# Key preparations, state reload, gated blocks and last root in other places, and the second mixer's fine levels on four 32-column tiles

## The chip, the cores and the metric

One core of a Trainium2 chip runs the whole program. The metric is the device time of one execution in microseconds; of several runs the median counts. TensorE (PE) multiplies, VectorE (DVE) and ScalarE (ACT) read its results out of PSUM banks and prepare operands, SyncE (SP) issues the loads of weights, and ScalarE issues most other DMAs from its own queue. Each engine works through its instructions in the order in which they were written; semaphores hold the engines together.

## The reference

One inference step of a decoder layer, for 512 prompt tokens and 8 x 8 sample tokens of width 1024, in fp32. Cut to what matters here:

```python
def gla_scan(q, k, v, la, S0):                 # second mixer, chunked
    def step(Sst, inp):
        Bc = jnp.cumsum(lac, axis=1)
        decay = jnp.exp(where(tril, Bc[:, :, None] - Bc[:, None, :], -inf))
        A = jnp.einsum('bthd,bshd,btshd->btsh', qc, kc, decay)
        o = einsum('btsh,bshv->bthv', A, vc) + einsum('bthd,bhdv->bthv', qc * exp(Bc), Sst)
        S_new = exp(BL)[..., None] * Sst + einsum('bshd,bshv->bhdv', kc * exp(BL[:, None] - Bc), vc)
...
def trunk(...):
    a = rmsnorm(h); z = a @ w_in                # all projections of both mixers
    hm = mlstm_scan(mq, mk, mv, li, lf)         # first mixer: matrix memory
    hg = gla_scan(gq, gk, gv, la, S0)           # second mixer: gated linear attention
    merged = sigmoid(ga) * (head_layernorm(hm) * sigmoid(mo) @ w_pa) + sigmoid(gb) * (head_rmsnorm(hg) * silu(gg) @ w_pb)
    h = h + merged @ w_o
    h = h + conv_ffn(rmsnorm(h))
    h = h + sigmoid(rmsnorm(h) @ w_ple_gate) * (p @ w_ple_proj)
    y = rmsnorm(h)
```

The outputs are the tokens and, for both mixers and the convolution, the states after the prompt and after the sample tokens.

## The kernel before

**Order.** `plan()` writes the whole order down as one list, `sched`. Its units are slices of weights: each is loaded by SP (`wraw`), split by ScalarE into a rounded high part (`whi`, L1841) and by VectorE into the rest (`wlo`, L1117, or in halves, L1125), and used by TensorE in tiles of 128 output features (or of 128 tokens for the values `mv`, `gv`). Each tile is three sums of fast products, high by high, low by high and high by low (L750 and, where the low weights are awaited first, L756; L859 and L865 for the values; L777 to L786 for the last projection). Between the tiles the list places stages, small steps of the mixers and norms. All engines walk the same list, and each does its part of a stage where it stands. The dictionaries in `plan()` say behind which tile of a unit a stage comes. Stages take jobs in the four PSUM banks of `aux`, in turn from `bank0`, except `m1`, which always takes banks 0 to 3; TensorE waits with `bank(j)` until the bank's last user has been read.

**First mixer.** A prompt chunk is 128 tokens (`c` 0 to 3; `NC` = 4 is the sample). `m1 c` makes key transposes, scores and spread rows on TensorE (L950 to L958), and VectorE and ScalarE weight them. `m2 c` multiplies keys by values (L969, VectorE adds to the state) and the scores by the values (L975, L979), which ScalarE copies out (L1917). For the sample rows `hpre`, `hout` and four `hk` update the states `st` in two pairs of heads: each `hk` takes all four banks (L1013), VectorE updates (L1784), and ScalarE stores that part of the state (L2112); for the first pair of a mixer it then reloads the part before with the next pair's state (L1912), after a wait for its store.

**Second mixer.** The decay between two tokens of a chunk is cut into levels of width 64, 32, ..., 1: at each level queries and keys are scaled relative to the middle of blocks of twice the width (`lsub`, `lmul`), and TensorE multiplies the early half of a block by the late one (`lev`, L1050 for 64, L1056 for the others, `gkt` L1032 for the diagonal). The levels go in pairs, four `lev` stages a chunk. Two 64 x 64 diagonal blocks, on two 64-column tiles of the array, hold all levels under 64; VectorE collects them through masks in `attd` (L1713), ScalarE copies `attd` into `att` (L2146), and `gout` multiplies by the values (L1066 to L1075).

**Gated blocks.** `bt m n` and `bt g n` transpose a mixer's output (L910, L912), gate it (VectorE L1808 to L1812, ScalarE L1879, L2168, VectorE L1178) and so make block n of the inputs of the units `pa` and `pb`. `pa`'s tiles are multiplied by their gate from PSUM (L1212).

**Last norm.** The last projection `pgate` runs over tokens 256 to 575, then over 0 to 255 (`PLE_ORDER`). `rsum 3` sums the squares of the first part, `rroot 3` takes the root (ScalarE L1844, VectorE L1149 to L1159) and `rspread 3` spreads it over the partitions (TensorE L717, L719). For tile g `evac` (L1297) takes the product out, `merge_ple` and `sum_square` handle the tile before, and `lo_half` (L1125) splits half a unit's weights.

## Time and profile before

| | us |
|---|---|
| median of 3 runs | 1207.81 |
| all runs | 1207.75, 1211.03, 1207.81 |
| profiled execution | 1210.15 |
| its span in the profile | 1208.4 |

| engine | busy us | share of the span |
|---|---|---|
| TensorE, products | 1184.1 | 98% |
| VectorE | 739.1 | 61% |
| ScalarE | 371.1 | 31% |
| GpSimd | 2.3 | 0% |

The span runs from the first to the last instruction; the profiled execution is some 2 us longer than its span, and above the median of the runs. TensorE's busy time is the union of its products, so overlapping ones count once. Every fp32 product stands in the trace as two passes, each with a weight load (PEld) of its own; those with rounded operands are one. All times below are us from the start of the span in the profiled execution.

### The profile page before, as it was taken

The page shows a single profiled execution, that of the slowest core. Times are in us where ns is not written, and L with a number is a line of the kernel's source. Part 1 is how long each engine was busy: PE and PEld are TensorE (multiplying, and loading weights), DVE is VectorE, ACT ScalarE, POOL GpSimd, SP SyncE. Part 2 cuts the span into 40 slices and gives each one's busy share as a digit, 9 for nine tenths or more (in the row PEclk, how much of TensorE's full clock was granted, in tenths as well). Part 3 has the DMA queues.
Part 4 walks back from the last instruction along what each step waited for, and adds up shares of the span by engine and source line. Part 5 has one row for each costly group of instructions (what it writes and reads, how often), then busy time and mean ns, then how long its engine had stood idle before and what let it go on. Part 6 is the DMA issues. An engine that isn't in the chain of part 4 may idle for free.

```text
span 1208.4 us, 21815 instructions
## 1 busy us (share of the span) xinstructions
PE 1184.1 (98%) x9289; PEld 1145.1 (95%) x9289; DVE 739.1 (61%) x1323; ACT 371.1 (31%) x506; POOL 2.3 (0%) x7
## 2 busy tenths in 40 slices
PE   9999999999999999999999999999999999999995
PEld 8999889999999999999899999999999999999995
DVE  6855467765877655564556566666676653323776
ACT  6233222232443422232333323322322321111543
POOL 0000000000000000000000000000000000000000
PEclk9999999999999999999999999999999999999997
DMA  6332411422132367454443541122222143223222
GB/s 215 107 141 73 154 53 59 170 71 90 65 100 93 106 228 238 167 182 137 126 153 101 192 164 71 71 75 100 71 89 87 59 142 123 71 92 96 91 81 79
DMA packets 48770, 138.45 MB, mean 115 GB/s; under 512 B 5365, under 2 KB 24949, under 8 KB 39585
## 3 DMA queue, kind: packets, MB, share of 16 engines
q1 hardware_dynamic: 16296, 89.39, 21.6%
q10 hardware_dynamic: 32376, 47.66, 11.6%
q8 instruction: 74, 1.21, 0.4%
q14 instruction: 24, 0.19, 0.0%
HBM read 113.15 MB, written 23.81 MB: 113 GB/s over the span
## 4 chain that ended last, share of the span: by engine, by line
PE 92%; issue 3%; DVE 2%; ACT 1%; DMA 1%; ACTq 0%; POOL 0%; POOLq 0%; DVEq 0%
PE ps L750 62%; PE ps L756 9%; PE ps L859 6%; PE ps L865 3%; PE ps L777 2%; PE aux L1056 1%; DMA xT<-in_xT 1%; PE aux L1013 1%; PE aux L1066 1%; PE aux L1003 1%; PE aux L1072 1%; PE aux L910 1%; PE aux L951 0%; PE aux L975 0%; PE aux L979 0%
## 5 line engine op out<-in xcount | busy, mean ns | idle before, releaser
L750 PE MATMUL ps<-ahi,whi 128*128 128x288 f32 x1536 | 332.6, 298 | 0.0
L750 PE MATMUL ps<-alo,whi 128*128 128x288 f32 x1536 | 329.5, 296 | 0.0
L750 PEld LDWEIGHTS ps<-ahi,whi 128*128 128x128 f32 x1536 | 247.5, 189 | 4.1 <-issue 1.2
L750 PEld LDWEIGHTS ps<-alo,whi 128*128 128x128 f32 x1536 | 246.6, 188 | 0.0
L1117 DVE TENSOR_TENSOR wlo<-wraw,whi 128x2048 fp32r<-128x2048 f32 (+1 forms) x82 | 176.0, 2147 | 79.2 <-ACT whi L1841 75.2
L1841 ACT ACTIVATE whi<-wraw 128x2048 fp32r<-128x2048 f32 (+1 forms) x87 | 156.5, 1799 | 154.2 <-PE ps L750 104.1
L750 PE MATMUL ps<-ahi,wlo 128*128 128x288 f32 x800 | 171.3, 296 | 0.0
L750 PEld LDWEIGHTS ps<-ahi,wlo 128*128 128x128 f32 x800 | 128.8, 189 | 0.0
L756 PE MATMUL ps<-ahi,wlo 128*128 128x288 f32 x736 | 105.5, 296 | 0.0
L756 PEld LDWEIGHTS ps<-ahi,wlo 128*128 128x128 f32 x736 | 100.7, 189 | 0.0
L750 PE MATMUL ps<-achi,whi 128*128 128x288 f32 x336 | 72.0, 296 | 0.0
L750 PE MATMUL ps<-aclo,whi 128*128 128x288 f32 x336 | 71.9, 296 | 0.0
L750 PE MATMUL ps<-achi,wlo 128*128 128x288 f32 x336 | 71.9, 296 | 0.0
L859 PE MATMUL ps<-whi,ahi 128*128 128x256 f32 x256 | 63.9, 287 | 0.0
L859 PE MATMUL ps<-whi,alo 128*128 128x256 f32 x256 | 62.7, 283 | 0.0
L750 PEld LDWEIGHTS ps<-achi,wlo 128*128 128x128 f32 x336 | 54.1, 189 | 0.0
L750 PEld LDWEIGHTS ps<-achi,whi 128*128 128x128 f32 x336 | 54.1, 189 | 0.0
L750 PEld LDWEIGHTS ps<-aclo,whi 128*128 128x128 f32 x336 | 54.1, 189 | 0.0
L1209 DVE TENSOR_TENSOR stg<-ps,rs 128x576 f32<-128x576 f32 x32 | 24.2, 757 | 44.2 <-PE ps L756 25.1
L859 PEld LDWEIGHTS ps<-whi,ahi 128*128 128x128 f32 x256 | 48.9, 191 | 2.4 <-issue 1.6
L859 PEld LDWEIGHTS ps<-whi,alo 128*128 128x128 f32 x256 | 49.0, 191 | 0.0
L1264 DVE TENSOR_TENSOR vrs<-ps,rsv 128x576 f32<-128x576 f32 x21 | 15.9, 756 | 44.3 <-PE ps L750 44.3
(385 smaller groups left out, 1699.3 us busy)
## 6 DMA issues: line engine op xcount, KB each, us to landing
wraw<-in_w_in SPq DMA_DIRECT2D x31, 1024.0 KB, 5.1
wraw<-in_w_up SPq DMA_DIRECT2D x21, 1024.0 KB, 4.8
gate_scratch<-stg ACTq DMA_DIRECT2D x32, 288.0 KB, 2.9
gt<-gate_scratch ACTq DMA_DIRECT2D x32, 288.0 KB, 3.0
wraw<-in_w_pgate SPq DMA_DIRECT2D x6, 1024.0 KB, 4.7
wraw<-in_w_down SPq DMA_DIRECT2D x8, 704.0 KB, 4.0
wraw<-in_w_down SPq DMA_DIRECT2D x8, 640.0 KB, 3.8
out_C_s<-st ACTq DMA_DIRECT2D x16, 256.0 KB, 2.9
```

What stands on the lines that cost most here:

```text
L750: mm = nc.tensor.matmul(ps[:, t % 2, a, 0:HALF], w, x(k)[:, a * HALF:(a + 1) * HALF], start=f, stop=e)
L756: mm = nc.tensor.matmul(ps[:, t % 2, a, 0:HALF], wlo[:, s, col:col + P], hi(k)[:, a * HALF:(a + 1) * HALF], start=False, stop=n == len(blo ...
L777: mm = nc.tensor.matmul(out, w, x[:, k, lo:hi], start=f, stop=e)
L859: nc.tensor.matmul(out, x[:, k] if x is not None else both_of(k), whi[:, w, k * DV:(k + 1) * DV], start=k == 0 and x is passes[0][0], stop ...
L865: mm = nc.tensor.matmul(out, x[:, k] if x is not None else both_of(k), wlo[:, w, k * DV:(k + 1) * DV], start=False, stop=k == KT - 1)
L910: mm = nc.tensor.transpose(b[:, c * L:(c + 1) * L], v[:, c, hd, c0:c0 + P], ident[:, :])
L1003: mm = nc.tensor.matmul(out[r0:r0 + 32, 0:wd], qb[:, e, g, 32 * i:32 * (i + 1)], st[e][:, 4 * g + i, 0:wd], start=False, stop=i == 3)
L1013: mm = nc.tensor.matmul(banks[r][:, 0:wd], k[rows, i, :], pair_of(which)[4][rows, v, 0:wd], start=n == 0, stop=n == 2)
L1117: V.tensor_tensor(wlo[:, s, 0:n], wraw[:, s, 0:n], f32(whi[:, s, 0:n]), ALU.subtract)\
L1209: V.tensor_tensor(two(stg[:, k % 2, :]), full, two(rs[:, :]), ALU.mult).then_inc(fr, 1)
L1264: V.tensor_tensor(two(vrs[:, :]), full, two(rsv[:, :]), ALU.mult).then_inc(fr, 1)
L1841: A.activation(whi[:, s, 0:n], wraw[:, s, 0:n], ACT.Copy).then_inc(split_hi, 1)
```

## The change

- Three `hk` stages of the first mixer's first pair come earlier among the value tiles: `hk 1` behind the last tile of `mv` 2, `hk 2` and `hk 3` behind the first two of `mv` 3. `m1 0`, the preparation of keys and scores of chunk 0, comes one tile later.
- The reloads of that pair's parts of the state are stages of their own, behind `m1 1` and `m1 2`. Each part of the state has its own semaphore for stores, four for each of the two buffers in place of two.
- `m2` starts at bank 0.
- In `pa` one `bt g` follows each tile; before, two followed the second.
- `rroot 3` stands ahead of tile 12 of the last projection, no longer behind it.
- In the second mixer the levels go 16, 8 / 4, 2 / 1, 64 / 32. For prompt chunks the diagonal and the levels under 32 are multiplied as four 32 x 32 blocks on four 32-column tiles of the array, four products a head for two. `attd` holds 32 columns a head, masked by `cmaskq`, which VectorE copies from `cmask` once. The results of levels 64 and 32 are copied into `att` by ScalarE, and `attd` is copied in four pieces once level 1 is in.

The sample chunk is as before. The core of the diff:

```diff
@@ -54,7 +55,7 @@
 V_BY_VECTOR = {"mv": (1, 3), "gv": (0, 1, 3)}
 UW = 2048
 NORM_MIX, NORM_M, NORM_G, NORM_FFN, NORM_PLE, NORM_OUT = range(6)
-PROMPT_LEVELS = [64, 32, 16, 8, 4, 2, 1]
+PROMPT_LEVELS = [16, 8, 4, 2, 1, 64, 32]
 SAMPLE_LEVELS = [4, 2, 1]
 ZMO, ZGG, ZGA, ZGB = 0, 8, 16, 24
 
@@ -112,10 +113,10 @@
     units_of("mk", 2, {0: [("rows", 1)], 1: [("rows", 2)], 3: [("rows", 3)]})
     unit("mv", 0, {h: [("la", h)] for h in range(H)})
     unit("mv", 1, {0: [("la_exp",)], 1: [("m1", NC)], 2: [("la_ln",)], 4: [("la_min",)]})
-    unit("mv", 2, {0: [("hpre", "m", 0)], 2: [("hout", "m", 0)], 3: [("hk", "m", 0, 0)]})
-    unit("mv", 3, {0: [("hk", "m", 0, 1)], 2: [("m1", 0)], 4: [("hk", "m", 0, 2)]})
-    units_of("gq", 2, {0: [("hk", "m", 0, 3), ("m2", 0), ("m1", 1)],
-                       1: [("m2", 1), ("tnorm", "m", 0), ("m1", 2), ("sload", 1)],
+    unit("mv", 2, {0: [("hpre", "m", 0)], 2: [("hout", "m", 0)], 3: [("hk", "m", 0, 0)], 4: [("hk", "m", 0, 1)]})
+    unit("mv", 3, {0: [("hk", "m", 0, 2)], 1: [("hk", "m", 0, 3)], 3: [("m1", 0)]})
+    units_of("gq", 2, {0: [("m2", 0), ("m1", 1), ("reload", 0), ("reload", 1)],
+                       1: [("m2", 1), ("tnorm", "m", 0), ("m1", 2), ("reload", 2), ("reload", 3)],
                        2: [("m2", 2), ("m1", 3)], 3: [("m2", 3), ("tnorm", "m", 1), ("la_scan", 0)]})
     units_of("gk", 2, {0: [("hpre", "m", 1), ("la_scan", 1)], 1: [("hout", "m", 1), ("la_scan", 2), ("tnorm", "m", 2)],
                        2: [("hk", "m", 1, 0), ("la_scan", 3)], 3: [("hk", "m", 1, 1)]})
@@ -148,8 +149,7 @@
     units_of("gb", 4, {0: [("hout", "g", 1)], 1: [("hk", "g", 1, 0)], 2: [("hk", "g", 1, 1), ("tnorm", "g", NC)],
                        3: [("hk", "g", 1, 2)], 4: [("hk", "g", 1, 3)], 5: [("bt", "m", 4), ("bt", "m", 5)],
                        6: [("bt", "m", 6), ("bt", "m", 7)]})
-    units_of("pa", 4, {0: [("bt", "g", 0)], 1: [("bt", "g", 1), ("bt", "g", 2)],
-                       **{n: [("bt", "g", n + 1)] for n in range(2, KT - 1)}})
+    units_of("pa", 4, {n: [("bt", "g", n)] for n in range(KT)})
     units_of("pb", 4, {})
     units_of("wo", 4, {})
     for i in range(FT):
@@ -158,7 +158,7 @@
         unit("down", i)
     unit("pproj", 0, {KT - 2: [("rsum", 2)]}, )
 
-    out = {11: [("rsum", 3)], 12: [("rroot", 3)], 13: [("rspread", 3), ("yout", 0)], 14: [("yout", 1), ("yout", 2)],
+    out = {11: [("rsum", 3)], 13: [("rspread", 3), ("yout", 0)], 14: [("yout", 1), ("yout", 2)],
            15: [("yout", n) for n in range(3, 5)]}
     for i in range(4):
         unit("pgate", i, {n: out.get(2 * i + n, ()) for n in range(2)}, before=(("rspread", 2),) if i == 0 else ())
@@ -171,7 +171,7 @@
         if i == 2:
             sched.append(("split", at[("pgate", 4)]))
     for i in (4, 5):
-        unit("pgate", i, {n: out.get(2 * i + 4 + n, ()) for n in range(2)})
+        unit("pgate", i, {n: out.get(2 * i + 4 + n, ()) for n in range(2)}, before=(("rroot", 3),) if i == 4 else ())
     sched += [("rsum", 4), ("rspread", 4)]
     return units, sched
 
@@ -253,6 +253,7 @@
 
 
         n = aux_jobs(s)
+        bank0 -= bank0 % 4 if s[0] == "m2" else 0
         for k in range(n):
             bank_of.append(3 - k if s == ("rspread", 0) else k if s[0] == "m1" else (bank0 + k) % 4)
@@ -1027,10 +1032,14 @@
                         pe.wait_ge(fm_ready, 4 * H)
                     b = bank(j)
                     for h in range(H):
-                        for e in range(2) if c < NC else (h % 2,):
-                            at_, t1 = (h * TS, t0 + TS * e) if c < NC else (h // 2 * TS, t0)
-                            mm = nc.tensor.matmul(b[half_of(e), at_:at_ + TS], gk[:, h, t1:t1 + TS],
-                                                  gq[:, h, t1:t1 + TS], start=True, stop=True)
+                        for e in range(4) if c < NC else ():
+                            t1 = t0 + QT * e
+                            mm = nc.tensor.matmul(b[quarter_of(e), h * QT:(h + 1) * QT], gk[:, h, t1:t1 + QT],
+                                                  gq[:, h, t1:t1 + QT], start=True, stop=True)
+                        if c == NC:
+                            at_ = h // 2 * TS
+                            mm = nc.tensor.matmul(b[half_of(h % 2), at_:at_ + TS], gk[:, h, t0:t0 + TS],
+                                                  gq[:, h, t0:t0 + TS], start=True, stop=True)
                     mm.then_inc(aux_ready, 1)
                     pe.wait_ge(kf_ready, c + 1)
                     b = bank(j + 1)
@@ -1049,6 +1058,13 @@
                             if w == TS:
                                 mm = nc.tensor.matmul(b[0:TS, h * TS:(h + 1) * TS], xl[:, h, 0:TS], xl[:, h, TS:],
                                                       start=True, stop=True)
+                                continue
+                            if c < NC and w < QT:
+                                for e in range(4):
+                                    late = xl[:, h, quarter_of(e)].rearrange("p (b s) -> p b s", s=2 * w)[:, :, w:]
+                                    mm = nc.tensor.matmul(b[quarter_of(e), h * QT // 2:(h + 1) * QT // 2]
+                                                          .rearrange("p (b s) -> p b s", s=w),
+                                                          xl[:, h, quarter_of(e)], late, start=True, stop=True)
                                 continue
                             for e in range(2) if c < NC else (h % 2,):
@@ -1679,8 +1698,8 @@
 
                     b = job(j)
                     if c < NC:
-                        i = V.copy_predicated(attd[:, :, :], bcast(cmask[:, 7, :], H, 1),
-                                              b[:, 0:H * TS].rearrange("p (h s) -> p h s", h=H))
+                        i = V.copy_predicated(attd[:, :, :], bcast(cmaskq[:, 7, :], H, 1),
+                                              b[:, 0:H * QT].rearrange("p (h s) -> p h s", h=H))
                     else:
                         for e in range(2):
...
@@ -1702,16 +1721,16 @@
                     c, g = s[1:]
                     ln = chunk_span(c)[1]
                     for n, w in enumerate(levels_of(c, g)):
+                        if c < NC and w >= QT:
+                            continue
                         b = job(j + n)
                         k = PROMPT_LEVELS.index(w)
 
                         def late(x):
                             return x.rearrange("p h (b s) -> p h b s", s=2 * w)[:, :, :, w:]
-                        if w == TS:
-                            i = V.tensor_copy(att[0:TS, :, TS:], b[0:TS, 0:H * TS].rearrange("p (h s) -> p h s", h=H))
-                        elif c < NC:
-                            i = V.copy_predicated(late(attd[:, :, :]), late(bcast(cmask[:, k, :], H, 1)),
-                                                  b[:, 0:H * TS // 2].rearrange("p (h b s) -> p h b s", h=H, s=w))
+                        if c < NC:
+                            i = V.copy_predicated(late(attd[:, :, :]), late(bcast(cmaskq[:, k, :], H, 1)),
+                                                  b[:, 0:H * QT // 2].rearrange("p (h b s) -> p h b s", h=H, s=w))
                         else:
                             for e in range(2):
                                 r = half_of(e)
@@ -1720,15 +1739,15 @@
                         free(i, j + n)
 
                         dve.wait_ge(aux_free[bank_of[j + n]], use_of[j + n])
-                    if c < NC and g == 3:
+                    if c < NC and g == 2:
                         dve.sem_inc(attd_ready, 1)
                     elif c == NC and g == 1:
                         dve.sem_inc(at_ready, 1)
...
@@ -1908,7 +1927,7 @@
 
                 src = ins["C_in"] if q < 2 else ins["S_in"]
                 for e in range(2):
-                    act.wait_ge(st_out[e][i % 2], 16 * (2 * (q - 1) + i // 2 + 1))
+                    act.wait_ge(st_out[e][i], 16 * q)
                     act.dma_start(st[e][:, i:NB:4, 0:DV], src[2 * (q % 2) + e, :, i:NB:4, :]).then_inc(st_in[e], 16)
 
             def copy_out(j, dst, src_p, wd):
@@ -2109,11 +2128,13 @@
                     act.wait_ge(st_new, 4 * q + i + 1)
                     dst = outs["C_s"] if which == "m" else outs["S_s"]
                     for e in range(2):
-                        act.dma_start(dst[2 * p + e, :, i:NB:4, :], st[e][:, i:NB:4, 0:DV]).then_inc(st_out[e][i % 2], 16)
-                    if p == 0 and i:
+                        act.dma_start(dst[2 * p + e, :, i:NB:4, :], st[e][:, i:NB:4, 0:DV]).then_inc(st_out[e][i], 16)
+                    if q == 2 and i:
                         state_reload(q + 1, i - 1)
                     if which == "m" and p == 1 and i == 3:
                         act.dma_start(outs["n"], nout[:, :, :]).then_inc(out_done, 16)
+                elif s[0] == "reload":
+                    state_reload(1, s[1])
                 elif s[0] == "sload":
                     if s[1] == 2:
                         state_load(2)
@@ -2140,11 +2161,26 @@
                         x = xl_buffer(c, g, n)[:, :, 0:ln].rearrange("p h (b s) -> p h b s", s=2 * w)
                         A.activation(x[:, :, :, 0:w], x[:, :, :, 0:w], ACT.Exp, scale=-1 / TAU)
                         A.activation(x[:, :, :, w:], x[:, :, :, w:], ACT.Exp, scale=1 / TAU).then_inc(xl_exp, 1)
-                elif s[0] == "lev" and s[1] < NC and s[2] == 3:
-                    act.wait_ge(attd_ready, s[1] + 1)
-                    for e in range(2):
-                        i = A.activation(att[half_of(e), :, half_of(e)], attd[half_of(e), :, :], ACT.Copy)
-                    i.then_inc(gat_ready, 1)
+                elif s[0] == "lev" and s[1] < NC and s[2] >= 2:
+                    c, g = s[1:]
+                    if g == 2:
+                        act.wait_ge(attd_ready, c + 1)
+                        for e in range(4):
+                            A.activation(att[quarter_of(e), :, quarter_of(e)], attd[quarter_of(e), :, :], ACT.Copy)
+                    k = j + levels_of(c, g).index(TS if g == 2 else QT)
+                    act.wait_ge(aux_ready, k + 1)
+                    b = aux[:, bank_of[k], :]
+                    if g == 2:
+                        A.activation(att[0:TS, :, TS:], b[0:TS, 0:H * TS].rearrange("p (h s) -> p h s", h=H), ACT.Copy)\
+                            .then_inc(aux_free[bank_of[k]], 1)
+                    else:
+                        for e in range(2):
+                            r = slice(TS * e, TS * e + QT)
+                            i = A.activation(att[r, :, TS * e + QT:TS * (e + 1)],
+                                             b[r, 0:H * QT].rearrange("p (h s) -> p h s", h=H), ACT.Copy)
+                        i.then_inc(aux_free[bank_of[k]], 1)
+                        act.wait_ge(aux_free[bank_of[k]], use_of[k])
+                        act.sem_inc(gat_ready, 1)
                 elif s[0] == "gout":
```

## Rows read from the trace of the kernel before

**Rows 1.** The page's first part: busy us, share, instructions of TensorE
```profile
PE 1184.1 (98%) x9289; PEld 1145.1 (95%) x9289; DVE 739.1 (61%) x1323; ACT 371.1 (31%) x506; POOL 2.3 (0%) x7
```

**Rows 2.** TensorE's waits: us in total, times, longest us
```profile
PE aux L717 <- DVE vrs L1159: 3.7, 1, 3.7
PE aux L950 <- ACT vm L1917: 2.6, 3, 1.7
...
PE aux L910 <- DVE bt_t L1811: 1.8, 2, 1.5
```

**Rows 3.** Stretches, TensorE: length, busy (count), granted clock, DMA share, GB/s
```profile
150.00:154.00 4.00, 3.46 (x24) 0.58 0.21 69
...
588.00:591.00 3.00, 3.00 (x14) 0.51 0.94 378
...
1187.30:1191.00 3.70, 3.70 (x18) 0.50 0.12 44
```

**Rows 4.** Weight loads of two lines: ns shortest, median, longest; first, last; forms
```profile
L1056 PEld LDWEIGHTS aux<-xl x408: 132/138/138, 271.2 to 426.1; 128*64 128x64 f32 x136
...
L1003 PEld LDWEIGHTS aux<-st,qb x128: 106/110/113, 111.7 to 496.3; 128*32 128x32 f32 x128
```

**Rows 5.** Timeline of TensorE, two groups of tiled products: start, length, line, tiles
```profile
111.71 1.95 PE L1003 MATMUL aux<-st,qb 128*32 128x257 f32 x32
113.58 0.39 PE L859 MATMUL ps<-whi,ahi 128*128 128x256 f32 x1
...
280.65 1.12 PE L1056 MATMUL aux<-xl 128*64 128x32 f32 x32
281.70 0.39 PE L859 MATMUL ps<-whi,both 128*128 128x256 f32 x1
```

**Rows 6.** Timeline of TensorE, first mixer, 144 to 169 us; idle before in brackets
```profile
144.40 1.98 PE L969 MATMUL aux<-vm,ktok 128*128 128x257 f32 x8 [1.01 <-DVE st L1784]
...
150.54 0.45 PE L950 MATMUL aux<-ident,mk 128*128 128x128 f32 x1 [1.69 <-ACT vm L1917]
...
154.26 0.40 PE L750 MATMUL ps<-ahi,whi 128*128 128x288 f32 x1
...
160.75 1.90 PE L969 MATMUL aux<-vm,ktok 128*128 128x257 f32 x8
...
166.66 0.33 PE L950 MATMUL aux<-ident,mk 128*128 128x128 f32 x1 [0.48 <-ACT vm L1917]
...
168.80 0.40 PE L750 MATMUL ps<-ahi,whi 128*128 128x288 f32 x1
```

**Rows 7.** Timeline of ScalarE at the first `m2`
```profile
148.58 1.90 ACT L1917 ACTIVATE vm<-aux 128x257 f32<-128x257 f32 x4 [4.69 <-PE aux L975]
```

**Rows 8.** Timelines of TensorE and VectorE, 562 to 587 us
```profile
562.12 0.27 PE L912 MATMUL aux<-ident,vg 64*128 64x64 f32 x1
...
586.26 3.21 PE L756 MATMUL ps<-hmhi,wlo 128*128 128x288 f32 x16 [2.15 <-DVE wlo L1117]
...
565.62 2.29 DVE L1117 TENSOR_TENSOR wlo<-wraw,whi 128x2048 fp32r<-128x2048 f32 x1
...
583.91 2.29 DVE L1117 TENSOR_TENSOR wlo<-wraw,whi 128x2048 fp32r<-128x2048 f32 x1
```

**Rows 9.** Timelines of ScalarE, VectorE and TensorE, 1180 to 1196 us
```profile
1180.85 0.21 ACT L1844 ACTIVATE stat<-stat 128x5 f32<-128x5 f32 x1
...
1182.97 1.23 DVE L1125 TENSOR_TENSOR wlo<-wraw,whi 128x1024 fp32r<-128x1024 f32 x1 [1.52 <-ACT whi L1841]
1184.11 0.18 DVE L1149 RECIPROCAL stat<-stat 128x5 f32<-128x5 f32 x1
...
1185.98 1.23 DVE L1125 TENSOR_TENSOR wlo<-wraw,whi 128x1024 fp32r<-128x1024 f32 x1
...
1195.27 0.42 DVE L1297 TENSOR_TENSOR sgp<-ps,rsv 128x256 f32<-128x256 f32 x1
...
1190.91 1.45 PE L786 MATMUL ps<-ehi,wlo 128*128 128x256 f32 x8
```

33 lines of the change are left out of this document (20 added, 13 removed).

## Prediction

> **What bounds the kernel now.** I read the page's engine shares first: TensorE is busy for 98% of the span [rows 1], so an edit counts only by the TensorE time that it removes, or by a wait of TensorE that it opens or closes. Then the list of TensorE's waits: they are few and name places, above all the second-last `rspread`, and `m1`, whose first transpose waits three times for ScalarE's copies of the first mixer's outputs [rows 2]. Then the granted clock by stretches: near 151, 589 and 1188 us it is about half, 1.2 instead of 2.4 GHz, and each time TensorE has just stood idle [rows 3]. A wait is thus paid twice. Between these places TensorE runs without gaps, the second mixer (270 to 412 us) included: there only its own work counts.
>
> **Fine levels on four column tiles.** Each fp32 product shows as two passes. Per prompt chunk the diagonal and five levels had 4 heads x 2 tiles x 2 passes = 16 passes each; now 4 x 4 x 2 = 32, of 32 columns and with half the moving columns. Four chunks make 24 such groups, 384 passes more. Is a pass of half the size on twice the tiles cheaper? Two levels, 32 passes, take 280.65 to 281.70, or 1.05 us: 33 ns a pass, 0.53 us a level [rows 5]. They are two 64-column tiles side by side, some 58 ns for a pass on each (their 32 passes less an end of 0.12 us). What sets this is the weight load: it lasts 138 ns for 64 columns and 110 for 32 [rows 4], so 32 columns are worth 27 ns, and 58 is 2 x 27 plus some 5. A tile of 32 columns should take a pass every 32 ns. Whether four such tiles run side by side is seen in `hout`: 32 passes with 257 moving columns take 1.87 us, 58 ns each [rows 5], where an undivided pass of that width takes 217 ns (8 passes in the 1.90 us at 160.75, less the tail of the last, [rows 6]). They do overlap fourfold. So four passes cost 32 ns, a group 8 x 32 = 0.26 us in place of 8 x 58 = 0.47: 0.21 saved, times 24 = 5.1 us. What no row shows is that TensorE is fed one pass each 8 ns for long. The bounds: fourfold overlap at no loss, 5.1 us saved; and the 33 ns of today for each pass whatever its size, 0.53 us lost per group, 12.7 us. I take the first, since the load and overlap rows are the nearest to the new form, and keep 12.7 as a rival.
>
> The other side of this edit is cheap. VectorE's predicated copies halve; the copies of the levels 64 and 32 and two more diagonal pieces go to ScalarE, some five short copies a chunk. ScalarE's queue has behind them the exponentials of the next level and a weight split, wanted one whole tile (6.4 us) later. Levels 16 and 8 come first and level 32 alone last, so less work stands between the last level and `gout`. `cmaskq` and the larger clearing add about 1 us of VectorE once, before the first chunk, under the value tiles. If that cover is short, it costs at most this 1 us; I take 0.
>
> Here a rule speaks against the change. Measured first: the smallest mean pitch over many passes in the trace is the 33 ns of [rows 5]. The Trainium skill, "TensorEngine Tiling (Array Packing)", section Performance Considerations, says that a matmul has about 60 cycles of overhead whatever its free size, and warns not to take the tiling factor from a dimension that is small already. By that page of the Trainium skill a pass is never under 25 ns, a group 0.8 us, and the part would lose some 8 us, as an estimate. No run here shows which holds for passes this small.
>
> **First mixer.** Moved: `hk m 0` 1 to 3 stand earlier, each after another tile; `m1 0` one tile later; `m2` starts at bank 0; the state reloads leave `hk` on ScalarE's queue and come after `m1`. Today `m2 0` waits 1.01 us for VectorE's state update of `hk 3`, starts at 144.40, and ends late because ScalarE issues two state stores and two reloads before it copies (its copies start at 148.58), and `m1 1` then waits 1.69 us [rows 6, 7]. It waits for the last of four copies, because bank 0 is the last that `m2` used: 1.90 us for the four. With `m2` starting at bank 0, the first copy releases it. At 150.54 the clock halves, so `m1 1` takes 3.72 us (to 154.26) where `m1 2` takes 2.14 (166.66 to 168.80) [rows 6]. From 144.40 to 154.26 are 9.86 us, plus 1.01 idle before: 10.87. After the change: 16 passes of 217 ns are 3.5, some 0.3 more for VectorE's four copies that free the banks, by estimate, and 2.14 for `m1 1`: 6.0. Saved 4.9. At `m1 2` and `m1 3` the 0.48 us of wait [rows 6] and the restart go, 0.65 each: 1.3. Against that, `hk 2` now comes one value tile (2.9 us) after `hk 1`, whose update VectorE must finish first; all four banks are in use. VectorE has the sample value piece ahead of it, which itself waits for ScalarE behind two DMA issues. I price it between 0 and the 1.01 us seen for the same reason, and take 0.8. The reload DMAs (eight issues) stand on ScalarE's queue ahead of `m2 1` and `m2 3`'s copies, one tile of cover, 6.4 us; their data are wanted some 40 us later. Without that cover `m1 2` waits as `m1 1` did, 1.69 us. Sum: 4.9 + 1.3 - 0.8 = 5.4 us; bounds 2.5 (the clock halves all the same, a copy is late) and 6.5.
>
> **Gated blocks.** `bt g 2` shares banks with `bt g 0`, which VectorE has not read yet: with one more block this is 1.8 us of wait in two places [rows 2]. The third block in the first unit puts VectorE behind, so that the low weights of `pa`'s third unit come late (their split starts at 583.91) and TensorE idles 2.15 us; then the clock halves [rows 3, 8]. From the end of the split before (565.62 + 2.29 = 567.91) to 583.91 VectorE has three blocks and two evacuations, 16 us; with two blocks the split comes some 4 us earlier, more than the 2.15 that it was late. What comes next late: the first tile of unit 1 now starts near 562.4, behind the products of `bt g 1`, has 32 high passes of 133 ns (a tile's 48 take 154.26 to 160.7, [rows 6]), and wants its low weights at 566.7; this split ends at 567.91 [rows 8]. So 1.2 us of wait appear. Before: the waits of 1.8 and 2.15, about 0.3 for getting under way again after them, and 1.7 for some 3.4 us at half clock, 6.0; saved 4.8, bounds 2.5 and 5.
>
> **Last root.** `rspread 3` waits 3.71 us (the longest wait, [rows 2]). The square root is there at 1181.06, but VectorE does a half split (1182.97) before the root chain (1184.11) [rows 9]. With `rroot 3` first, the chain of 1.4 us ends at 1182.5, and TensorE goes on 3.0 us earlier. Behind the root's wait now stand the evacuation of tile 12, its merge and both half splits; the second ends at 1187.2 as today (1185.98 + 1.23). Tile 14 wants it for its low products at about 1185.6 and waits 1.6. They start at 1187.3 instead of 1190.91 [rows 9], 3.6 earlier. Then VectorE is late: its merges and outputs after that split take as long as now, so the last evacuation moves from 1195.27 [rows 9] to 1192.45. Saved 2.8 us; if the clock stays low, 1.2.
>
> **Sum.** 5.1 + 5.4 + 4.8 + 2.8 = 18.1 us. The profiled execution took 1210.15 us (span 1208.4); less 18.1 is 1192.0. It is 2.3 us above the median of the runs, 1207.81, about what one stretch at half clock costs (1.7 us), so the median run may have one fewer to lose: 1207.81 - 16.4 = 1191.4. I forecast **1191.5**.
>
> **Rivals.** (a) The waits move rather than go: TensorE, ahead by 1 to 5 us, meets VectorE or ScalarE at the next place (splits, state updates), and one stretch at half clock stays. Half of the 13.0 us of placement is lost: 1198. For: VectorE has no slack at 567.9 and 1187.2. Against: it waits for TensorE in most stages. (b) The feed rival: a pass costs its 33 ns whatever its size. The fine levels lose 12.7 instead of gaining 5.1, which is 17.8 us: 1209, no change. By the Trainium skill's 25 ns a pass (the section above) it would be near 1205. (c) Slower: the 32-column tiles do not overlap at small widths, the order of the passes on one tile making each wait for its own load. Then a pass takes 58 ns as on one 64-column tile, a group 1.87 us against 0.47, 24 x 1.4 = 33.6 us lost against 13.0 gained: 1228. It decides from about 0.47 + 13.0/24 = 1.01 us a group, 32 ns a pass. The fourfold overlap in `hout` speaks against it. (d) The placements bring little because the clock halves at other places too: 1203 to 1208.
>
> **How the numbers follow.** Forecast 0.60, (a) 0.22, (b) 0.08, (c) 0.04, (d) 0.06. The forecast's own range is 1187 to 1196. The bounds add: all at their best, 1186; (a) and the milder part of (d) reach 1203. Range 1186 to 1203, with 0.15 outside. 0.3%, 3.6 us, is about what can be told from no change. Faster: forecast, (a) and 0.04 of (d), 0.86. Within: 0.07 of (b) and the rest of (d), 0.09. Slower: (c) and 0.01 of (b), 0.05.
>
> **What would show it.** Two fine levels take about 0.6 us in place of 1.05, and a chunk's small products 1.3 us less; 1 us or more for the pair is (b). `m2 0` starts right behind its tile, `m1 1` to 3 have no wait for ScalarE, and the clock is full near 151 and 589. One wait of about 1.2 us for the low weights near `pa`'s second unit, none in its third. `rspread 3` waits under 1 us, and a new wait of 1 to 2 us for a split stands before the last 32 products of the projection. The prediction is wrong if a small pass is not paid by its columns, or if these waits come back elsewhere.

## The result, and the profile after

| | before | after |
|---|---|---|
| median of 4 runs each | 1208.76 us | 1200.34 us (1199.91 to 1200.77) |
| ratio | | 0.993, 95% interval 0.9918 to 0.9941 |
| profiled execution, its span | 1210.15, 1208.4 us | 1199.91, 1197.9 us |
| repeated beside the experiments | 1210.24 us | 1200.12 us, ratio 0.9919 (0.9906 to 0.9933) |

The change is faster by 0.7 to 0.8%, where the prediction had 1191.5 us, 1.4%. The time lies inside its range, the direction is right, and half of the gain is missing. Beside the experiments two executions of the kernel before took 1900.44 and 2040.62 us at mean clocks of 0.555 and 0.735 of full; the ratios are of the other runs alone. The page's first part shows that TensorE is still the bound, and its waits show what is left of those of [rows 2]. The first block is the profile page's row on the engines, the second the list of its waits (us in total, times, longest).

```profile
PE 1174.2 (98%) x9673; PEld 1135.1 (95%) x9673; DVE 734.5 (61%) x1319; ACT 376.5 (31%) x526; POOL 2.3 (0%) x7
```

```profile
PE aux L1082 <- ACT att L2179: 4.3, 3, 1.5
PE aux L707 <- DVE acc L1347: 2.4, 1, 2.4
...
PE ps L791 <- DVE wlo L1141: 1.5, 1, 1.5
PE ps L761 <- DVE wlo L1133: 1.1, 1, 1.1
...
PE aux L722 <- DVE vrs L1175: 0.7, 1, 0.7
PE aux L1018 <- DVE st L1803: 0.7, 1, 0.7
```

The longest wait of before, 3.7 us at the second-last `rspread` (L717 of before, L722 now), is down to 0.7. The three waits for ScalarE's `vm` copies and the two for `bt_t` are gone. Three waits were foretold and are there: 1.5 us for the half split (L791), 1.1 for the low weights of `pa`'s second unit (L761), 0.7 for the state update at `hk` (L1018). The first row was not foretold: three times TensorE stands at a ktok product of `gout` (L1082) for ScalarE's copies of the level 32. The second row, the wait ahead of the last sums of squares, was 1.6 us in before and is 2.4 in `root_alone` too: with the last root earlier, VectorE is the late one at the end.

The clock, by stretches of TensorE (length, busy and count, granted clock, DMA share, GB/s), the same stretches as [rows 3]:

```profile
150.00:154.00 4.00, 4.00 (x43) 1.00 0.20 62
588.00:591.00 3.00, 3.00 (x24) 1.00 0.30 99
1187.30:1191.00 3.70, 1.23 (x9) 0.78 0.24 89
```

In this execution the two stretches at half clock (1.2 GHz) near 151 and 589 us are gone. Near the end the clock is low only after TensorE has nearly run out of work.

The TensorE timeline at the first chunk's fine levels (start, length, line, tiles, count), to set against [rows 5]:

```profile
264.48 0.46 PE L1037 MATMUL aux<-gq,gk 128*32 128x32 f32 x32
264.87 0.66 PE L1047 MATMUL aux<-ident,kf 128*128 128x128 f32 x4
265.45 0.74 PE L1065 MATMUL aux<-xl 128*32 128x16 f32 x64
266.12 0.39 PE L864 MATMUL ps<-whi,ahi 128*128 128x256 f32 x1
```

Two levels, now 64 passes, take from 265.45 to 266.12: 0.67 us where 32 passes took 1.05. That is 10.5 ns a pass. TensorE does take a pass every 10 ns, for 64 in a row.

How far the ends of TensorE's tiles moved, from one profiled execution to the other (places by their time in before), gives the balance:

| stretch | shift | forecast |
|---|---|---|
| to the start of the first mixer, 119 us | +0.3 | 0 |
| first mixer, 119 to 190 us | -5.6 | -5.4 |
| second mixer, 190 to 418 us | +1.1 | -5.1 |
| 418 to 561 us (second state output) | +0.3 | 0 |
| `pa`, 561 to 623 us | -3.5 | -4.8 |
| last projection, 1172 to 1192 us | -3.9 | -2.8 |
| behind the last tile | +0.8 | 0 |
| sum (with rounding) | -10.5 | -18.1 |

Two of these shifts hold clock that not every execution of the old order loses. `levels_alone`, `blocks_alone` and `root_alone` (next section) have the order of before at `m1 1`. TensorE waits there as long as in before, but its clock stays full, and the stage takes 2.14 us where before took 3.72 (150.54 to 154.26, [rows 6]). The rows of `levels_alone`, and its stretch from 150 to 154 us:

```profile
150.78 0.33 PE L955 MATMUL aux<-ident,mk 128*128 128x128 f32 x1 [1.67 <-ACT vm L1936]
...
152.92 0.52 PE L755 MATMUL ps<-ahi,whi 128*128 128x288 f32 x2
```

```profile
150.00:154.00 4.00, 3.22 (x36) 1.00 0.26 82
```

So 1.6 us of the -5.6 are a loss that the one profiled execution of before happened to have. In the same way its clock was low for 6.8 us near 1185 us, and for 3.4 us in the profiled executions of `levels_alone`, `mixer_alone` and `blocks_alone`, which have the last root of before: 1.2 of the -3.9 us. Against executions at the same clock the first mixer gains 4.0 us and the last projection 2.7.

The second mixer alone is 6.2 us short. There the trace shows a chain over three engines. First comes ScalarE, second chunk (start, length, engine, line, operation, idle time before in brackets):

```profile
320.58 1.27 ACT L2169 ACTIVATE att<-attd 32x128 f32<-32x128 f32 x4 [1.37 <-DVEq L1743]
321.86 0.38 ACT L2174 ACTIVATE att<-aux 64x256 f32<-64x256 f32 x1
322.25 1.28 ACT L2162 ACT_TABLE_LOAD   x1
323.55 0.42 ACT L2162 ACTIVATE xl<-xl 128x256 f32<-128x256 f32 x1
...
327.97 0.33 ACTq L2012 DMA_DIRECT2D gate_scratch<-stg  x1
328.34 0.54 ACT L2179 ACTIVATE att<-aux 32x128 f32<-32x128 f32 x2 [4.07 <-DVE stg L1225]
```

Then VectorE and TensorE in the same view:

```profile
324.31 0.42 DVE L1693 TENSOR_TENSOR xl<-xl,gk 128x256 f32<-128x256 f32 x1 [3.08 <-ACT xl L2163]
...
324.98 2.28 DVE L1133 TENSOR_TENSOR wlo<-wraw,whi 128x2048 fp32r<-128x2048 f32 x1
...
327.19 0.75 DVE L1225 TENSOR_TENSOR stg<-ps,rs 128x576 f32<-128x576 f32 x1
...
328.94 0.70 PE L1082 MATMUL aux<-vg,ktok 128*128 128x256 f32 x2 [1.43 <-ACT att L2179]
```

To be read down: ScalarE copies five pieces (1.65 us), then loads its table for the exponentials (1.28 us), and VectorE stands 3.08 us for them. Its split of 2.28 us and the eviction of the tile come late. ScalarE's store of that tile waits for the eviction, and behind the store in its queue stand the two copies of the level 32, which free the bank that the fourth ktok product wants. In the first chunk ScalarE loads no table at this place, VectorE stands 1.80 us instead of 3.08, and TensorE does not wait (what the table load costs by itself was not tried):

```profile
287.81 0.43 DVE L1693 TENSOR_TENSOR xl<-xl,gk 128x256 f32<-128x256 f32 x1 [1.80 <-ACT xl L2163]
```

### The profile page after: what moved, and what is told of

It is laid out like the page before. It is cut to its first block, busy times and chain, and to the rows that moved or that the text cites. A ratio compares the mean times of both kernels' runs of the same rounds, so it can differ in the third digit from the quotient of the medians.

```text
span 1197.9 us, 22605 instructions
## 1 busy us (share of the span) xinstructions
PE 1174.2 (98%) x9673; PEld 1135.1 (95%) x9673; DVE 734.5 (61%) x1319; ACT 376.5 (31%) x526; POOL 2.3 (0%) x7
## 4 chain that ended last, share of the span: by engine, by line
PE 86%; DVE 6%; issue 4%; ACT 3%; DMA 1%; ACTq 1%; POOL 0%; DVEq 0%; POOLq 0%
PE ps L755 58%; PE ps L761 8%; PE ps L864 6%; PE ps L870 3%; PE ps L782 2%; DVE wlo L1133 1%; DMA xT<-in_xT 1%; PE aux L1018 1%; PE aux L980 1%; PE aux L1008 1%; DVE stg L1225 1%; PE aux L974 1%; PE aux L1088 1%; PE aux L915 0%; DVE xl L1693 0%
## 5 line engine op out<-in xcount | busy, mean ns | idle before, releaser
L761 PE MATMUL ps<-ahi,wlo 128*128 128x288 f32 x736 | 105.6, 296 | 0.0
L761 PEld LDWEIGHTS ps<-ahi,wlo 128*128 128x128 f32 x736 | 100.7, 189 | 0.0
```

The lines of the kernel that those rows point to most:

```text
L761: mm = nc.tensor.matmul(ps[:, t % 2, a, 0:HALF], wlo[:, s, col:col + P], hi(k)[:, a * HALF:(a + 1) * HALF], start=False, stop=n == len(blo ...
```

## The experiments

The theory from this trace, T1: the levels themselves gain about 4 us, and ScalarE's copies ahead of its exponentials cost 5, by that chain. Rivals: the waits come from how moved parts and levels meet (T0); only the place of the level-32 copies behind the store counts (T2); the turn of the banks does, as the level 32 is now alone in its group (T3).

**The two halves of the change.** `levels_alone` is the kernel before with the levels, their order and ScalarE's copies; `places_alone` is the kernel before with all else of the diff. Their edits are parts of the diff shown.

> The kernel before with the four-tile levels alone: quarter products, new order of the levels, copies by ScalarE; nothing else is moved. The prediction's sum gives it -5.1 us against before. Theory T1 (read from the changed kernel's trace: the levels save TensorE some 4 us, and ScalarE's new copies in front of its table load hold VectorE up, so that the fourth ktok product of chunks 1, 2 and 3 waits 1.4 to 1.5 us for its bank, 1.65 us of lost time each): the same three waits at the product into aux from vg and ktok, and a total of -4 + 5 = about +1 us, between 1208.0 and 1211. Rival T0 (the waits come only from how the moved parts and the levels meet): no such waits, about 1204.

> The kernel before with all that is moved and without the levels: key preparations, reload, bank alignment, gated blocks, last root. The prediction's terms give -5.4 - 4.8 - 2.8 = -13.0 us against before, 1195.8. Theory T1 (the shortfall is mostly in the second mixer; the moved parts give what the shifts between the two traces show, -5.5 - 3.6 - 3.1 and +0.4 at the second state output): -11.8 us, about 1197, so some 3 us faster than the kernel with all of the change. Rival T0 (the parts need each other, or the moved parts are what fell short): -7 to -9 us, 1200 to 1202, and with it the levels would be worth what is left.

Measured: `levels_alone` 1209.91 us against 1209.49, ratio 1.0005 (0.9995 to 1.0015). `places_alone` 1198.90 us, ratio 0.9916 (0.9902 to 0.9930). So the levels, forecast at -5.1 us, brought nothing by themselves, and the moved parts make up the gain of the whole change. TensorE's longest waits in `levels_alone` are:

```profile
PE aux L1082 <- ACT att L2177: 4.4, 3, 1.5
PE aux L722 <- DVE vrs L1175: 3.7, 1, 3.7
```

The three waits at the ktok products are there without any moved part: T0 is out. In the shifts against before, this kernel loses 1.97 us from the second chunk to the fourth (308 to 418 us), as the whole change does (1.97 there too). `places_alone` does not decide by itself: at 1210 us its ratio is -10.2 us (-11.9 to -8.5), between T1's -11.8 and T0's -7 to -9. The waits in `levels_alone` decide.

**ScalarE's five copies behind the exponentials, `late_copies`.** The copies of `lev c 2` are put into a function `att_copies`, and:

```
 elif s[0] == "lsub":
...
         A.activation(x[:, :, :, w:], x[:, :, :, w:], ACT.Exp, scale=1 / TAU).then_inc(xl_exp, 1)
+    if c < NC and g == 3:
+        att_copies(c, 2)
...
-elif s[0] == "lev" and s[1] < NC and s[2] >= 2:
+elif s[0] == "lev" and s[1] < NC and s[2] == 3:
```

> The changed kernel, in which ScalarE makes its five copies of level group 2 (four of attd, one of the 64 level) behind the exponentials of level group 3 instead of ahead of them. Theory T1 (copies and then the table load delay the exponentials, those VectorE's products, its weight split and its tile eviction, behind which ScalarE's store and its two copies of the 32 level stand): the exponentials start 1.6 us earlier, VectorE's wait of 3.1 us falls to about 1.5, the waits of 1.4 us at the fourth ktok product fall under 0.3, and the time falls by 3.5 to 5 us to about 1196. T2 (only the place of the two 32-level copies behind the store counts, whatever VectorE does): the store moves with VectorE's eviction, so a part goes, 1 to 2 us. T3 (the turn of the banks: the 32 level is now one job and shares its bank with the fourth ktok product, and any ScalarE copy is too late for it): the waits stay above 1 us, within 1 us of the changed kernel.

**The two copies of level 32 ahead of the store, `copies_first`.**

```
 elif kind in ("mo", "gg", "ga", "gb"):
...
+    if s in lev3_after:
+        att_copies(lev3_after[s], 3)
     act.wait_ge(tile_free[tt % 2], tt // 2 + 1)
     act.dma_start(zs[k, :, :], stg[:, k % 2, :]).then_inc(stg_out[k % 2], 16)
```

(`lev3_after` holds, for each tile, the chunk whose level 32 comes right behind it.)

> The changed kernel, in which ScalarE makes its two copies of the 32 level ahead of the store of the tile before them instead of behind it; the copies of level group 2 stay where they are. T2 (only the place behind the store counts): the waits at the fourth ktok product go and nothing takes their place, -4.5 to -5 us, 1195.5. T1 (VectorE is late in any case): the copies run 2 us earlier and free the bank in time, but VectorE frees the bank of the first ktok product only after its late eviction, and the product of att into that bank waits 0.3 to 0.8 us in chunks 1, 2 and 3: -2.5 to -4 us, 1197. T3 (the turn of the banks): as T2 here. If both this and late_copies take all of the waits away, either edit alone is enough and the cause is the chain as a whole.

Measured: `late_copies` 1196.65 us, ratio 0.9896 (0.9879 to 0.9913), 3.5 us below the changed kernel's 1200.12; `copies_first` 1198.34 us, ratio 0.9910 (0.9895 to 0.9925), 1.8 below it. Each ratio is to the kernel before beside it, whose median was 1209.49 us here and 1210.24 beside the repeated change, so 0.7 us of both differences may be the base. In the traces, where this does not enter, the tile ends from 308 to 418 us shift by 5.0 us from the changed kernel to `late_copies`. Some 1.7 us of that is lost again in its profiled execution to half clock at two places that the edit does not touch: 0.9 us near 26 us (last section) and 0.8 in the last sums of squares. In `late_copies` the row at L1082 is gone from the waits. Its timeline of ScalarE and VectorE in the second chunk is:

```profile
321.52 1.28 ACT L2184 ACT_TABLE_LOAD   x1 [1.36 <-DVE stg L1225]
322.82 0.42 ACT L2184 ACTIVATE xl<-xl 128x256 f32<-128x256 f32 x1
...
323.45 1.25 ACT L1939 ACTIVATE att<-attd 32x128 f32<-32x128 f32 x4
...
323.57 0.43 DVE L1693 TENSOR_TENSOR xl<-xl,gk 128x256 f32<-128x256 f32 x1 [1.40 <-ACT xl L2185]
```

VectorE stands 1.40 us instead of 3.08, 1.68 less, which is the 1.65 us of copies. In `copies_first` VectorE stands as long as before, ScalarE's copies run 2.4 us earlier, and TensorE waits at the next step, for VectorE's state update:

```profile
325.90 0.55 ACT L1951 ACTIVATE att<-aux 32x128 f32<-32x128 f32 x2 [1.74 <-PE aux L1072]
...
328.36 0.67 PE L1088 MATMUL aux<-vg,att 128*128 128x256 f32 x2 [0.58 <-DVE gst L1757]
```

That is the wait that T1 expected (0.3 to 0.8 us in three chunks). T2 expected none here, and no more than 2 us gained in `late_copies`; T2 is out. In time it gave less than T1's 2.5 to 4 us; by the tile ends from 308 to 418 us it is 2.7. T3 is out: both kernels keep the turn of the banks.

**Only the level 64 moved, `level64_late`.** As `late_copies`, but the four copies of `attd` stay in `lev c 2`: a dose of 0.38 us of the 1.65.

> The changed kernel with only the copy of the 64 level (0.38 us) behind the exponentials of level group 3; the four copies of attd (1.27 us) stay ahead of them. late_copies moved all five and gained 3.7 us (waits of 1.43 us gone). Theory T1 (a chain without slack: each 0.1 us ahead of the exponentials is 0.1 us of wait): the waits fall by 0.38 each to about 1.05, together 1.1 us faster than after_again, 1199.1. Rival R (a threshold: the table load behind any copies is what hurts): the waits stay at 1.4, the time that of after_again within 0.4 us.

Measured: 1199.35 us, ratio 0.9914 (0.9900 to 0.9927), 0.8 us below the changed kernel. The medians alone do not tell it from no change; the wait does. It is now

```profile
PE aux L1082 <- ACT att L1945: 3.3, 3, 1.2
```

1.0 to 1.1 us less in three chunks for 0.38 us of copies taken away in each, and the tile ends from 308 to 418 us shift by 1.2 us. That is a chain without slack in these three chunks, as T1 says, and no threshold.

**The moved parts one by one.** Each is its part of the diff on the kernel before.

> The kernel before with the first mixer's part alone: key preparations, m1 0, bank alignment of m2, state reloads. The prediction's term is -5.4 us. Theory T1 (this term held in the shifts between the traces, -4.1 at m1 1 and -1.4 behind it, and the second state output then waits 0.4 us longer): -5.1 us, about 1204.4, clock full near 151 us. Rival R (the two other stretches at half clock and their waits move with it, so that what it gains is partly lost at the gated blocks): -2 to -3 us.

> The kernel before with the gated blocks of the fourth projection, one a tile, alone. The prediction's term is -4.8 us (new wait 1.2 us at the second unit). Theory T1 (the changed kernel's trace: TensorE's gaps at the low weights of units 1, 2 and 3 are 1.40, 0.41 and 0.43 us where the usual pitch is 0.13, since VectorE's split stands behind the block in every unit; only the first was in the prediction): -3.6 us, 1205.9. Rival R (the part needs the others' timing): within 1 us of no change or over -5.

> The kernel before with the last root ahead of the half split, alone. The prediction's term is -2.8 us, with 1.2 if the clock stays low near the end. The shifts between the two traces behind the root are -3.1 to -3.9 us and the clock no longer halves between 1184.8 and 1191.7: -3.3 us, 1206.2. Rival R: the stretch at half clock stays, -1.2 us.

| kernel | us | ratio (95%) | change | forecast |
|---|---|---|---|---|
| `mixer_alone` | 1205.24 | 0.9961 (0.9948 to 0.9973) | -4.7 | -5.4 |
| `blocks_alone` | 1205.76 | 0.9968 (0.9955 to 0.9981) | -3.9 | -4.8 |
| `root_alone` | 1207.06 | 0.9978 (0.9968 to 0.9988) | -2.7 | -2.8 |
| `levels_alone` | 1209.91 | 1.0005 (0.9995 to 1.0015) | +0.6 | -5.1 |
| sum | | | -10.7 | -18.1 |
| whole change, repeated | 1200.12 | 0.9919 (0.9906 to 0.9933) | -9.8 | |

The changes are worked out from the ratios at 1210 us. The parts add up to the whole within its interval of 8.1 to 11.4 us. The rivals of the mixer and the root do not fit: the first gains over 3 us, the second more than 1.2. For the blocks the interval, 2.3 to 5.4 us, just reaches the rival's 5; by the tile ends from 561 to 623 us they gain 3.1 alone and 3.5 in company, so they hardly need the other parts. The list of waits of `root_alone` shows the block waits of [rows 2] unchanged and those of the tail as in the whole change. The second state output, which shifted by 0.3 us and which T1 had put down to the first mixer, shifts over the same stretch (418 to 561 us) by 0.2 in `blocks_alone` and 0.4 in `root_alone`, where nothing ahead of it is edited: this is a difference between executions and not of the change.

> The changed kernel once more, unedited, so that its time stands beside these runs of the kernel before on one chip. The medians so far: changed kernel 1200.3, parts alone -4.7 (mixer), -4.0 (blocks), -2.7 (root) and about +0.6 (levels), sum -10.8; the moved parts together -10.2. Theory T1 (levels lose what their copies cost, the rest adds up): a ratio of 0.991 to 0.993, 1199 to 1201. Rival R (the levels cost more in company than alone): above 0.993.

It measured 1200.12 us, as T1 expected.

**What the gated blocks still leave: `late_split_first`.** The trace after shows VectorE's split behind each block of `pa`, and TensorE just behind the split (first the second unit, with its wait, then the split of the third unit, whose products L761 start at 578.94):

```profile
561.73 2.29 DVE L1133 TENSOR_TENSOR wlo<-wraw,whi 128x2048 fp32r<-128x2048 f32 x1
...
564.07 0.81 PE L761 MATMUL ps<-hmhi,wlo 128*128 128x288 f32 x4 [1.10 <-DVE wlo L1133]
...
576.60 2.29 DVE L1133 TENSOR_TENSOR wlo<-wraw,whi 128x2048 fp32r<-128x2048 f32 x1
```

On top of `late_copies`:

```
-ahead = n == late and (kind, i) in (("gb", 3), ("pa", 3))
+ahead = n == late and (kind == "pa" or (kind, i) == ("gb", 3))
```

> late_copies (the changed kernel with ScalarE's five copies behind the exponentials), and besides the low-weight split of each unit of the fourth projection ahead of that tile's gated block on VectorE instead of behind it. Theory T1 of the gated blocks (the split stands behind the block, whose last step itself waits 0.9 us for ScalarE): the gaps of 1.40, 0.41 and 0.43 us at the low weights all fall to 0.13, so 1.8 us against late_copies' 1196.65, 1194.8. Rival R (TensorE then meets the late block instead: the products of the next block wait for the banks that VectorE has not read): waits of 0.5 us or more at the block's products, and less than 0.7 us gained.

Measured: 1193.11 us, ratio 0.9862 (0.9848 to 0.9876). The waits at L761 are gone and none has come at the blocks. Now the split starts 5.6 us ahead of the products that want it:

```profile
553.33 2.29 DVE L1133 TENSOR_TENSOR wlo<-wraw,whi 128x2048 fp32r<-128x2048 f32 x1
...
558.93 2.30 PE L761 MATMUL ps<-hmhi,wlo 128*128 128x288 f32 x16
```

By the last tile the shift against `late_copies` is 2.1 us, and the medians differ by 3.5. Of the rest, 0.8 us stands behind the last tile, where the last sums of squares ran at half clock in the profiled execution of `late_copies` and at full clock here. What is left, 0.6 us, fits the stretch near 26 us of the last section: both profiled executions have it at half clock, but the mean clocks of this kernel's other runs are higher. That is argued, not shown.

**Two claims on the first mixer,** each tried on `late_split_first`. `no_align` takes out the line that starts `m2` at bank 0; `reloads_back` issues the reloads inside `hk` again:

```
-bank0 -= bank0 % 4 if s[0] == "m2" else 0
```

```
-units_of("gq", 2, {0: [("m2", 0), ("m1", 1), ("reload", 0), ("reload", 1)],
-                   1: [("m2", 1), ("tnorm", "m", 0), ("m1", 2), ("reload", 2), ("reload", 3)],
+units_of("gq", 2, {0: [("m2", 0), ("m1", 1)],
+                   1: [("m2", 1), ("tnorm", "m", 0), ("m1", 2), ("reload", 3)],
...
-if q == 2 and i:
+if p == 0 and i:
     state_reload(q + 1, i - 1)
```

> late_split_first without the bank alignment of m2, all else the same. The prediction took the first transpose of m1 1 to wait for the last of ScalarE's four copies (1.90 us) and the alignment to let it go on with the first. If so, waits of TensorE for ScalarE's vm copies come back at m1 1, 2 and 3, about 1.4, 0.5 and 0.5 us, and with them +2.4 us, or +4.1 with a stretch of 3.4 us at half clock (1.7 us): 1195.5 to 1197.2. Rival R (what helped was that nothing stands ahead of the copies on ScalarE any more): no wait above 0.5 us and under 0.7 us slower, 1193.5.

> late_split_first with the state reloads issued by ScalarE inside hk again (the reload of piece i-1 behind the stores of piece i), all else the same. The prediction counted the reloads among what delays ScalarE's copies at m2 0. Theory T1 (what counted was hk 3 directly ahead of m2 0; two tiles earlier the reloads are issued before the copies are wanted): the copies of m2 0 start with TensorE's products as now, no new wait, within 0.7 us of 1193.1. Rival R (the reloads wait for the stores to land and hold ScalarE's queue): its weight splits come late, new waits at whi or vm of over 1 us, 1194.5 or more.

Measured: `no_align` 1194.77 us, ratio 0.9878 (0.9864 to 0.9891), 1.7 us slower than with the alignment; by the tile ends 0.7 us at each of `m1` 1 to 3. Its wait is

```profile
PE aux L954 <- ACT vm L1957: 1.4, 3, 0.5
```

three of about 0.5 us, where the expectation was 1.4, 0.5 and 0.5 and at least 2.4 us in all: ScalarE copies while the products still run, so only the end of the last copy is waited for. `reloads_back` took 1193.96 us, ratio 0.9867 (0.9854 to 0.9881), 0.9 us slower; the two intervals overlap, so the trace has to tell. It shows a new wait of TensorE of 1.0 us at the start of a value tile, for ScalarE's copy of a value tile before it. That copy and the weight split ahead of it stand behind the first pair of reloads, 1.32 us on ScalarE's queue:

```profile
126.22 1.32 ACTq L1931 DMA_DIRECT2D st<-in_C_in  x2
127.64 1.91 ACT L1860 ACTIVATE whi<-wraw 128x2048 fp32r<-128x2048 f32 x1 [5.23 <-DVEq L1810]
129.58 0.47 ACT L2023 ACTIVATE vm<-ps,rscol 128x256 f32<-128x256 f32 x1
...
130.11 0.39 PE L864 MATMUL ps<-whi,ahi 128*128 128x256 f32 x1 [0.96 <-ACT vm L2023]
```

So it lies between the two expectations. ScalarE's copies of `m2 0` were not delayed; the reloads' place is worth some 0.7 to 0.9 us, by another wait than the one that the prediction named. If the two edits add, they are 2.7 to 2.9 us of the 4.0 that the first mixer gains at the same clock. What is left goes with the earlier `hk 3`, above all the wait of 1.01 us for VectorE's update ahead of `m2 0` [rows 6]; that was not run by itself.

## Why the prediction was right and wrong

**The bound, right.** TensorE at 98% before and after, and each us gained or lost sits at a wait of TensorE or in its own work.

**The levels on four column tiles, wrong by 5.7 us (alone) to 6.2 us (in the balance), of 7.6 us that the whole is short there.** The part that looked risky held: the 33 ns a pass of [rows 5] were no price of a pass. The new form takes 10.5 ns, so rivals (b) and (c) are out. The size was a little off, since 8 ns a pass had been taken: a group of 32 passes takes 0.34 us, not 0.26, and what it saves is less. Read alike (busy 0.74 for two levels against the 1.12 of [rows 5], 0.19 each) 24 groups give 4.6 us; between `places_alone` and `late_copies` the tile ends shift by 4.0 us (the medians differ by 2.3; the rest is the two places at half clock named at `late_copies`). The forecast was 5.1. The step that failed is the sentence "The other side of this edit is cheap", with its claim that what stands behind ScalarE's copies is wanted one whole tile later, and the price of 0, with 1 us as the most that it could cost. What stands behind them is the exponentials, for which VectorE was standing already, with a split, the eviction of the tile, and through ScalarE's store again ScalarE's last copies behind it. In the last three chunks the cover was not 6.4 us but none: 1.65 us of copies became a wait of 1.4 to 1.5 us at TensorE and 1.65 us lost in each of them, 4.9 us, and the tile ends give 5.0. Only the first chunk had cover. `late_copies` removed the loss by changing one order, and `level64_late` a quarter of it by a quarter of the copies. Rival (a), waits that move rather than go, is what happened; but it was argued for the placements and its price (half of 13.0 us) was put there, and it was the levels that paid. The cost of `cmaskq` and the larger clearing, taken at 0, is at most 0.2 us: so much the kernels with the levels lose once, ahead of the first chunk, and `places_alone` does not.

**First mixer, right in size, in part by luck:** -5.6 us in the tile ends, -4.7 (-6.3 to -3.3) alone, forecast -5.4. The term counts 1.6 us for the half clock behind the wait at `m1 1`, and the prediction says that a wait is thus paid twice. With the same wait, one of four profiled executions had the half clock there, before's, and three had not; without it the gain is 4.0 us. The wait of 1.69 us of [rows 6] is gone, and the transposes follow the products:

```profile
144.44 1.90 PE L974 MATMUL aux<-vm,ktok 128*128 128x257 f32 x8
...
148.27 0.27 PE L955 MATMUL aux<-ident,mk 128*128 128x128 f32 x1
```

The 0.8 us taken for `hk 2` measured 0.7 (L1018), the 3.8 us forecast for the products measured 3.83 (148.27 - 144.44). The causes were weighed wrongly in part: the alignment is worth 1.7 to 2.0 us over three chunks and 0.7 of it at the first wait, where the prediction let it remove the wait for all four copies.

**Gated blocks, right in kind, 0.9 to 1.3 us too high.** The foretold wait of 1.2 us at the second unit measured 1.1, and the clock stays full. The prediction stopped there and said that no wait stands in the third unit. In the two units behind, the low products start 0.41 and 0.43 us after the passes before them where 0.13 is usual: too short for the list of waits, 0.6 us together. VectorE gets the split done only just in time in every unit, since it stands behind a block that itself waits for ScalarE. `late_split_first` got 2.4 us in the tile ends for all three units, of which 2.1 are left at the last tile. 0.3 to 0.7 us of the shortfall stays open.

**Last root, right:** -2.7 us alone, forecast -2.8. The foretold wait of 1.6 us for the half split measured 1.5, that at `rspread` 0.7 (under 1 foretold):

```profile
1175.18 0.70 PE L722 MATMUL aux<-vrs,ones 128*128 128x256 f32 x2 [0.71 <-DVE vrs L1175]
...
1179.84 1.21 PE L791 MATMUL ps<-ehi,wlo 128*128 128x256 f32 x8 [1.50 <-DVE wlo L1141]
```

TensorE gains 3.9 us here and the end 3.1, since VectorE is the last, as forecast: its last tile eviction goes from 1195.27 [rows 9] to 1184.82, 10.45 earlier, of which 7.4 come from the stages before. In both, 1.2 us is the longer stretch at half clock in the profiled execution of before, so against executions at the same clock it is 2.7 and 1.9 us; the interval of `root_alone`, 1.5 to 3.9 us, holds the forecast and both.

**The base.** 1207.81 us was the median of three runs; the later ones of the kernel before gave 1209.49 to 1210.24. The pair that gave the result had 1208.76 us before, so 1 us of the 8.8 between 1191.5 and 1200.34 is the base. That the profiled execution of before had more half clock than others, as the prediction's sum supposes, the rows of `levels_alone`, `blocks_alone` and `root_alone` at `m1 1` bear out.

**The range** held the time, because (a) had been priced at 1198 and the milder half of (d) at 1203, and not because the chain was foreseen; that is luck. Its lower end does not follow from the bounds: all terms at their best save 1.3 us more than the forecast, about 1190 us and not 1186.

## What to carry to other kernels

When work is handed to an engine that is busy 31% of the time, the price is not read from its share but from what stands behind the new work in its queue, and from who is already waiting for that. Follow the chain over all engines back to the bound: here 1.65 us of copies went through exponentials, products, a split, an eviction, a store and two copies, and came out at TensorE as the same 1.65 us. Two rows of VectorE's timeline of before, in the same chunk, would have hinted at it:

```profile
329.62 0.43 DVE L1674 TENSOR_TENSOR xl<-xl,gk 128x256 f32<-128x256 f32 x1 [1.07 <-ACT xl L2142]
...
332.70 0.76 DVE L1209 TENSOR_TENSOR stg<-ps,rs 128x576 f32<-128x576 f32 x1
```

VectorE already stands idle for ScalarE's result, and its next eviction waits for nobody, so the delay passes on. The first sign alone is not enough: in the first chunk of before VectorE stands idle for ScalarE too (0.82 us), but its eviction then waits 1.54 us for TensorE:

```profile
297.93 0.76 DVE L1209 TENSOR_TENSOR stg<-ps,rs 128x576 f32<-128x576 f32 x1 [1.54 <-PE ps L750]
```

That is slack, and in that chunk of the changed kernel the same copies cost TensorE no wait.

## What the runs showed of the hardware beyond the expected

A weight load and product on four 32-column tiles can follow each other every 10.5 ns, for 64 passes in a row. The page "TensorEngine Tiling (Array Packing)" of the Trainium skill, section Performance Considerations, puts about 60 cycles of overhead on each matmul; worked out in the prediction as an estimate of 25 ns a pass, that is more than twice what the rows at 265.45 and 266.12 show. As a pitch over all passes it does not hold here. Each of the four tiles gets a pass every 42 ns, so these rows do not speak against it for one tile.

TensorE's clock near 26 us is full in some executions and half in others, after the same idle of 0.7 to 0.8 us, in kernels that are the same up to there: of the fourteen profiled executions eight have it full, those of before and after among them, and six half, those of `late_copies` and `level64_late` among them. The stretch from 26 to 30 us of TensorE, first of before, then of `level64_late`:

```profile
26.00:30.00 4.00, 3.84 (x23) 1.00 0.00 0
```

```profile
26.00:30.00 4.00, 4.00 (x17) 0.62 0.00 0
```

It costs about 1 us from there on: the shift at 119 us against before is 1.19 us in `late_copies`, 0.27 in the changed kernel and -0.16 in its repeat. The clock behind the wait of 1.69 us at `m1 1` differs in the same way (1.6 us, see the balance). So two kernels that differ by 1 us are not told apart by one profiled execution each, and shifts are to be read stretch by stretch, with the clock beside them. What makes the clock fall in one execution and not in another after the same wait stays open.
